# Token sums of squares added on VectorE, and another order around the layer norm, in a two-block model kernel

## The reference

```python
def rms_norm(x, gain):                      # also _rmsnorm
    return x * rsqrt(mean(x * x, -1) + 1e-6) * gain

# first block: 16 meta tokens are put ahead of the 512, so L = 528
hn = rms_norm(h, attn_norm)
h = h + fox_mixer(hn)                       # attention, 16 heads of 64, gated; ends with o @ w_out
h = h + (silu(n @ W_gate) * (n @ W_up)) @ ffn_w_out     # n = rms_norm(h, ffn_norm), hidden 2816
x = rms_norm(h, final_norm)[:, 16:]

# second block: c gives six vectors sh1, sc1, g1, sh2, sc2, g2 through w_ada
n1 = _rmsnorm(x, norm1_g) * (1 + sc1) + sh1
glu_in, z, xbc, dt_raw, gate_in = split(n1 @ w_in)
u_a, u_b = split(glu_in); u = u_a * sigmoid(u_b)
u = silu(_layernorm(causal_depthwise_conv(u, 31 taps)))  # subtract the token's mean, scale by rsqrt(var + eps)
y_cv = u @ w_cv_out
xbc = silu(causal_depthwise_conv(xbc, 4 taps))           # 2048 columns xs, 512 B, 512 C
y = ssd(xs, softplus(dt_raw + dt_bias), -exp(a_log), B, C) + d_skip * xs   # 32 heads, 4 groups, chunks of 64
y = _rmsnorm(y * silu(z), per group of 512)
g_cv, g_ssm = split(sigmoid(gate_in))
x = x + g1 * ((g_cv * y_cv + g_ssm * (y @ w_ssm_out)) @ w_mix_out)
n2 = _rmsnorm(x, norm2_g) * (1 + sc2) + sh2
x = x + g2 * moe(n2)                        # 64 experts of hidden 512 in 8 groups, top 2
return _rmsnorm(x, final_g)
```

## Time and profile before

| | before |
|---|---|
| time, median of 3 runs | 2719.16 us (2712.14 to 2720.99) |
| time of the profiled execution | 2708.46 us |
| its span | 2706.6 us |
| mean granted TensorE clock | 0.939 of full speed |
| busy: PE / DVE / ACT / POOL | 89% / 31% / 28% / 28% |
| chain that ended last, by engine | PE 56%, DMA 27%, DVE 10%, ACT 4%, issue 1% |
| its largest lines | DMA arena<-in_w 21%, L734 11%, L736 11%, L735 11%, L1240 7%, L2102 4%, L789 3% |
| DMA, mean over the span | 221 GB/s |
| DMA in slices 26 to 39 of 40 | 422 to 426 GB/s |

### The profile page before, as it was taken

The page is one execution under the profiler, slowest core; times in us unless marked ns, Lnnn a source line. Parts: engine busy times, 40 slices in busy tenths (PEclk is TensorE's granted clock), DMA queues, the critical chain, the costliest instruction groups (busy, mean ns, idle before and its releaser), DMA issues.

```text
span 2706.6 us, 27116 instructions
## 1 busy us (share of the span) xinstructions
PE 2417.0 (89%) x11252; PEld 1513.6 (56%) x11252; DVE 828.7 (31%) x1354; ACT 753.4 (28%) x1201; POOL 767.2 (28%) x487
## 2 busy tenths in 40 slices
PE   8999789999999998689997998798888888888885
PEld 6677457778888786577776786332222222332221
DVE  1633551100003799316654422311111111111113
ACT  4433552322223333236655422200000000000001
POOL 3333443454543443143322461401001010011000
PEclk9999899999998999699998899899999999988997
DMA  4253212532323332132333325799999999999995
GB/s 166 100 185 126 76 36 94 173 122 78 125 70 101 94 94 86 44 124 95 109 125 129 150 96 225 267 423 426 426 426 426 426 426 426 424 424 424 425 422 215
DMA packets 165051, 597.33 MB, mean 221 GB/s; under 512 B 15875, under 2 KB 81411, under 8 KB 139328
## 3 DMA queue, kind: packets, MB, share of 16 engines
q1 hardware_dynamic: 148320, 562.23, 53.3%
q10 hardware_dynamic: 5936, 23.90, 2.3%
q0 software_dynamic: 10672, 9.46, 1.1%
HBM read 591.01 MB, written 28.96 MB: 229 GB/s over the span
## 4 chain that ended last, share of the span: by engine, by line
PE 56%; DMA 27%; DVE 10%; ACT 4%; issue 1%; POOL 0%; SPq 0%; ACTq 0%; DVEq 0%; POOLq 0%
DMA arena<-in_w 21%; PE ps L734 11%; PE ps L736 11%; PE ps L735 11%; PE ps L1240 7%; DVE ps L2102 4%; DMA ring<-in_w 3%; PE ps L789 3%; PE ps L1238 2%; PE ps L1259 2%; ACT arena L1342 1%; DMA ring<-in_w_ada 1%; PE ps L818 1%; PE ps L808 1%; PE ps L761 1%
## 5 line engine op out<-in xcount | busy, mean ns | idle before, releaser
L2497 POOL TENSOR_TENSOR ring_r<-ring,ring_r 128x1024 fp32r<-128x1024 f32 (+2 forms) x220 | 514.2, 2342 | 802.9 <-ACT ring_r L1331 802.8
L734 PE MATMUL ps<-r,ring_r 128*128 128x512 f32 (+1 forms) x1552 | 622.5, 401 | 9.7 <-ACT arena L1342 4.9
L735 PE MATMUL ps<-r,ring_r 128*128 128x512 f32 (+1 forms) x1552 | 610.8, 394 | 0.0
L736 PE MATMUL ps<-r,ring_r 128*128 128x512 f32 (+1 forms) x1552 | 610.6, 393 | 0.0
L1342 ACT ACTIVATE arena<-ps 128x512 f32<-128x512 f32 (+4 forms) x279 | 187.9, 693 | 1234.9 <-PE ps L1240 868.8
L1240 PE MATMUL ps<-arena 128*64 128x512 f32 x672 | 326.7, 644 | 79.5 <-DMA arena<-in_w 79.4
L734 PEld LDWEIGHTS ps<-r,ring_r 128*128 128x128 f32 (+1 forms) x1552 | 294.3, 190 | 81.5 <-issue 18.7
L1238 PE MATMUL ps<-arena 128*64 128x512 f32 x672 | 332.9, 644 | 0.0
L735 PEld LDWEIGHTS ps<-r,ring_r 128*128 128x128 f32 (+1 forms) x1552 | 294.2, 190 | 65.2 <-issue 3.7
L736 PEld LDWEIGHTS ps<-r,ring_r 128*128 128x128 f32 (+1 forms) x1552 | 293.5, 189 | 64.6
L1331 ACT ACTIVATE ring_r<-ring 128x1024 fp32r<-128x1024 f32 (+2 forms) x220 | 222.8, 1014 | 332.4 <-PE ps L736 231.0
(11 more groups left out here) (329 smaller groups left out, 2370.9 us busy)
## 6 DMA issues: line engine op xcount, KB each, us to landing
arena<-in_w SPq DMA_DIRECT2D x105, 2048.0 KB, 35.9
ring<-in_w SPq DMA_DIRECT2D x87, 2048.0 KB, 37.1
ring<-in_w_ada SPq DMA_DIRECT2D x12, 2048.0 KB, 12.8
ring<-in_ffn_w_in SPq DMA_DIRECT2D x22, 1024.0 KB, 7.7
ring<-in_w_in SPq DMA_DIRECT2D x40, 512.0 KB, 5.8
ring<-in_fox_w_in SPq DMA_DIRECT2D x8, 2048.0 KB, 8.2
ring<-in_w_in SPq DMA_DIRECT2D x8, 2048.0 KB, 9.6
ring<-in_ffn_w_out SPq DMA_DIRECT2D x4, 2048.0 KB, 7.9
```

Source lines behind the costliest of these rows:

```text
L734: e.matmul(out, wh[:, k, :], X.hi[:, k0 + k, :], start=first and k == 0, stop=False)
L735: e.matmul(out, wh[:, k, :], X.lo[:, k0 + k, :], start=False, stop=False)
L736: m = e.matmul(out, wl[:, k, :], X.hi[:, k0 + k, :], start=False, stop=last and k == nk - 1)
L2497: e.tensor_tensor(GL[t], grans[t][1], GH[t].bitcast(F32), ALU.subtract).then_inc(sem["gr_lo"], 1)
```

## The change

- **Squares added up by VectorE.** For all of these norms VectorE adds the rows of squares elementwise (`add_squares`, L1853) into one row, `ACC[0]` (which is `RST`), except the last. TensorE then does one `sums_by_token`: for each 128 tokens the accumulated row and the last row of squares against ones, 8 matmuls instead of 32 (24 instead of 64 for "fin" with accumulators `RST` and `CBM`). The sums no longer stand between the tiles of op, of the feed-forward block's output and of n2. Row k's squares wait for the add of row k - 2.
- **ada(8)** stands after op5 instead of after op7.
- **The output weights of the feed-forward block** come in four loads of 256 columns for each half instead of two of 512 columns split by rows, and the tiles follow: both parts (k 0 to 7, 8 on) of a tile behind each other instead of four tiles' first parts and then their second parts.
- **The start.** SyncE issues the first half (256 columns) of the first weight load before the input rows have landed, the second half after both.
- **Around the layer norm.** The last step's 4-tap convolution (xbc 6 and 7) runs ahead of the last 31 taps. All six gate tiles eg0 to eg5 stand on TensorE ahead of conv_sum 6 and 7; behind these xbc 8 and 9 ahead of the sums of "ln", xbc 10 around the spread, xbc 11 after it, then the transposes sb and the pair co0 and co1. The mean is evicted to a buffer of its own (`MEAN`, in CBM). The scans of dt stand behind the adds.

The diff, cut to its core ("..." marks what is left out; the other norms' calls change like those shown):

```diff
--- before.py
+++ after.py
@@ bank_table: the banks from the taps on (the other stages alike) @@
     t("eg", 0, skip=held)
+    t("eg", 1, skip=held)
     t("acc", skip=held)
-    t("eg", 1, skip=held)
+    for nt in range(2, NG):
+        t("eg", nt, skip=held)
+    t("xbc", 8)
+    t("xbc", 9)
+    t("ln")
+    t("xbc", 10, skip={ps("ln").bank})
+    t("lnb")
...
@@ weight_table @@
-        for c in range(2):
-            block(a["ffn_w_out"], 512 * c, r0=128 * k0)
-            block(a["ffn_w_out"], 512 * c, r0=128 * (k0 + 8), nk=n - 8)
+        for c in range(4):
+            ap = load((0, (n, 256), wrows(a["ffn_w_out"], 128 * k0, n, 256 * c, 256)))[:, :n * 256].rearrange("p (k n) -> p k n", k=n)
+            for j in range(2):
+                for k in (slice(0, 8), slice(8, n)):
+                    grans.append((len(loads) - 1, ap[:, k, 128 * j:128 * j + 128]))
...
     tiles(*[8224 + 128 * i for i in range(4, NG)])
+    block(a["w_in"], 4096)
     for c in range(2):
         block(a["w_cv_out"], 512 * c)
...
@@ build_program @@
+        ACC = [RST, CBM[:, 0:512]]
+        MEAN = CBM[:, :]
...
+        def square_of(name, k, i=0):
+            return ACC[i] if k == 0 else TMP[i if name == "fin" else k % 2]
...
@@ pe @@
-            def sum_row(name, j, nk, off=0):
...
-                for tt in range(4):
-                    rows = TMP[j % 2][:, off + 128 * tt:off + 128 * tt + 128]
...
+            def sums_by_token(name, off=0):
+                rows0, adds0, nk = sums[name]
+                many = n_sums.get(name, 1)
+                u = ps(*name) if type(name) is tuple else ps(name)
+                w.wait_ge(sem["sq"], rows0 + many * nk)
+                w.wait_ge(sem["sq_used"], adds0 + many * (nk - 2))
+                w.wait_ge(u.free, u.n)
+                both = [[square_of(name, k, i) for k in (0, nk - 1)] for i in range(many)]
+                for tt in range(4):
+                    at = slice(off + 128 * tt, off + 128 * tt + 128)
+                    for x in both[0]:
+                        m = e.matmul(u.ap[:, tt:tt + 1], x[:, at], ones[:, 0:1], start=x is both[0][0], stop=x is both[0][1])
+                    if many == 2:
...
             for nt in range(8):
                 whole("op", nt, X=XO)
-                if nt % 4 == 3:
-                    ada(7 + nt // 4)
-                if nt >= 2:
-                    sum_row("fn", nt - 2, 8)
-            sum_row("fn", 6, 8)
-            sum_row("fn", 7, 8)
+                if nt in (3, 5):
+                    ada(7 + nt // 5)
+            sums_by_token("fn")
...
-                for c in range(2):
-                    for r in (0, 8):
-                        for j in range(4):
-                            u = ps("fo", half, 4 * c + j)
+                for c in range(4):
+                    for j in range(2):
+                        u = ps("fo", half, 2 * c + j)
+                        for r in (0, 8):
                             tile(u.ap, XH[half], u, k0=r, first=r == 0, last=r == 8)
...
             whole("eg", 0, X=X1)
+            whole("eg", 1, X=X1)
             conv_sum(4)
             conv_sum(5)
...
-            whole("eg", 1, X=X1)
+            for nt in range(2, NG):
+                whole("eg", nt, X=X1)
+            conv_sum(6)
+            conv_sum(7)
+            whole("xbc", 8, X=X1)
+            whole("xbc", 9, X=X1)
+            sums_by_token("ln")
+            whole("xbc", 10, X=X1, between={2: lambda: spread("ln", "lnb")})
+            whole("xbc", 11, X=X1)
             u = ps("sb")
...
-            whole("eg", 2, X=X1)
+            pair([ps("co", 0), ps("co", 1)], XC)
             ub, u = ps("sb"), ps("sc")
...
-            conv_sum(6)
-            conv_sum(7)
-            whole("eg", 3, X=X1)
-            sum_rows("ln", 8)
-            fill(2, "lnb")
-            spread("ln", "lnb")
-            whole("eg", 4, X=X1)
-            whole("eg", 5, X=X1)
-            pair([ps("co", 0), ps("co", 1)], XC)
             for nt in range(2, 8):
                 whole("co", nt, X=XC)
...
-            for j in range(4):
-                whole("xbc", 8 + j, X=X1)
             for g in range(4):
...
@@ act @@
-            def square_row(name, k, src, n, gain=1.0):
-                rows0, sums0 = sums[name]
-                if k >= 2:
-                    w.wait_ge(sem["sq_used"], sums0 + k - 1)
-                e.activation(TMP[k % 2][:, :n], src, ACT.Square, scale=gain).then_inc(sem["sq"], 1)
+            def square_row(name, k, src, n, i=0, gain=1.0):
+                rows0, adds0, nk = sums[name]
+                if name == "fin":
+                    if k >= 2:
+                        w.wait_ge(sem["sq_used"], adds0 + 2 * (k - 2) + i + 1)
+                elif k >= 3:
+                    w.wait_ge(sem["sq_used"], adds0 + k - 2)
+                e.activation(square_of(name, k, i)[:, :n], src, ACT.Square, scale=gain).then_inc(sem["sq"], 1)
...
+            for nt in range(NG):
+                early_gate(nt)
+            evict(MEAN, ps("red"), ACT.Copy, scale=1.0 / D)
...
@@ dve @@
+            def add_squares(name, k, n=T, i=0):
+                rows0, adds0, nk = sums[name]
+                many = n_sums.get(name, 1)
+                w.wait_ge(sem["sq"], rows0 + many * k + i + 1)
+                if k >= 2:
+                    w.wait_ge(sem["sq_used"], adds0 + many * (k - 2) + i + 1)
+                acc = ACC[i][:, :n]
+                e.tensor_tensor(acc, acc, square_of(name, k, i)[:, :n], ALU.add).then_inc(sem["sq_used"], 1)
...
+                if q == 3:
+                    short_conv(2 * q, [Cf[:, nt - 4, :] for nt in pair], accs)
+                    w.wait_ge(sem["xbc"], 8)
                 for i in range(31):
...
-            for c in range(4):
-                sl = slice(c * 128, (c + 1) * 128)
-                e.tensor_tensor_scan(DT[:, 2, sl], C("ones", 0, 32), DT[:, 1, sl], 0.0, ALU.mult, ALU.add).then_inc(sem["acs"], 1)
             u = ps("red")
...
             for k in range(8):
-                e.tensor_tensor(cv[:, k, :], cv[:, k, :], RST[:, :T], ALU.subtract).then_inc(sem["cvc"], 1)
...
+                e.tensor_tensor(cv[:, k, :], cv[:, k, :], MEAN, ALU.subtract).then_inc(sem["cvc"], 1)
+                if k >= 2:
+                    add_squares("ln", k - 1)
...
@@ sp @@
-            for i in range(3):
-                w.wait_ge(sem[f"in{i}"], 16)
...
+            (dst, src), = loads[0].parts
+            e.dma_start(dst[:, :, 0:256], src[:, :, 0:256]).then_inc(loads[0].slot, 16)
+            for i in range(3):
+                w.wait_ge(sem[f"in{i}"], 16)
+            w.wait_ge(loads[0].slot, 16)
+            e.dma_start(dst[:, :, 256:512], src[:, :, 256:512]).then_inc(loads[0].slot, 16)
```

More of the change, by code:

```diff
@@ L134, in state_tiles @@
 def state_tiles():
-    out = [("xbc", 8 + j) for j in range(4)]
+    out = []
     for g in range(4):
@@ L215, in bank_table @@
             t("fo", half, nt)
-            if half == 1 and nt == 4:
-                t("fin")
+    t("fin")
     t("finb")
@@ L454, in granule_uses @@
             whole("hu", nt)
-        for c in range(2):
-            for _ in range(4):
-                partly()
-            for j in range(4):
-                whole("fo", half, 4 * c + j)
+        for nt in range(8):
+            partly()
+            whole("fo", half, nt)
     for q in range(4):
@@ L466, in granule_uses @@
         whole("eg", nt)
+    for nt in range(8, 12):
+        whole("xbc", nt)
     for nt in range(8):
@@ L724, in granule, with tile @@
                 return t, GH[t], GL[t]
-            def tile(out, X, use, k0=0, first=True, last=True):
+            def tile(out, X, use, k0=0, first=True, last=True, between={}):
                 t, wh, wl = granule()
```

208 lines of the change are left out of this document (103 added, 105 removed).

## The result

The changed kernel takes 2672.08 us (median of four runs, 2671.10 to 2675.39), the kernel before beside it 2715.65 (2709.91 to 2720.99): a ratio of 0.9841, interval 0.9821 to 0.9860, some 43 us less. (Less than 2%, but clear of the noise.) The forecast was 2672.0. That the two agree to a tenth is chance: the profiled executions, from the first of which the sum was read, took 2708.46 and 2671.73, so they are 36.7 apart where the sum said 47.0, and the kernel before varies by itself (2705 to 2725 in all runs beside the experiments, with medians of 2711 to 2719). What follows goes by the traces.

What follows compares the result with a forecast made beforehand. A chain of waits bounds the kernel: TensorE's products, VectorE's taps, then expert loads. Terms 4.2 + 1.2 + 0 + 38.7 + 0 + 2.9 = 47.0 us off the median give 2672, range 2652 to 2695.

Steps and rivals of the forecast that it cites:

- What a saved us is worth: Stages ahead of the expert loop: what they save moves the whole loop, one for one; a 38.84 us stall stands there.
- Start: First norm, "x": root at about 18.5 instead of 22.67, inputs delayed by 2.5; gain 4.2 us (2 to 7).
- Output projection: Norm "fn": 4.1 us of squares out, new wait of 3 to 4.5 for ada(8)'s load; +1.2 (-1.5 to +2.5).
- fin: End of the feed-forward block: 8.5 us of rows out, longer tail at the lower clock; taken as 0, between -0.4 and +4.9.
- Layer norm: Convolution to state space stage: mean 13.9 us earlier, sums 1.8 us, pair co0, co1 34.0 earlier at 1126.0.
- xbc 11 to 1125.4: After the layer norm's sums: TensorE runs xbc 10 to 1120, xbc 11 to 1125.4, then the pair at 1126.0.
- Behind co7: Third z tile 38.8 us after co7 instead of 43.9, 5.1 saved; with the pair's part, gain 38.7 us (33 to 42).
- no needed cover: Rival denied: without the xbc tiles behind co7 TensorE idles and its clock halves; gain 20 us, 2699, chance 0.03.
- gn: Groups of the state space stage: fewer passes, but an add in the chain; 0 us (-3 to +4).
- n2: The norm "n2": 4.1 us of squares out, tail 1.2 longer for the last add; +2.9 us (0 to 4).
- The point figure: Whole kernel: 2672 us, the summed gain of 47.0 taken from the median of the runs shown.
- The case named the likeliest: Whole kernel: the forecast itself, gains of 33 to 56 us, chance 0.60.

Runs made afterwards that it cites:

- sp_late: Changed kernel with the first half of the first weight load issued behind the inputs' landing again, as before the change: 2670.42 us.
- fin_fill: Changed kernel with twelve filler matmuls where TensorE idles ahead of the token sums of "fin": 2671.69 us.
- pool3: Changed kernel with GpSimd splitting three granules (xbc 11, co0, co1) ahead of its low parts of the layer norm's rows instead of behind: 2660.57 us.
- xbc11_late: pool3 with xbc 11 moved from between the spread and the pair co0, co1 to behind co7: 2654.88 us.
- after_again: The changed kernel itself, run and profiled once more on the same chip as the variants: 2672.10 us (2667.61 to 2679.13).
- ada_first: Changed kernel with ada(8) left behind op5 but its load ahead of the first piece of the feed-forward weights in SyncE's list: 2662.93 us.
- start_root: xbc11_ada with the first weight load behind the inputs and ScalarE's granule copies behind the root: 2654.66 us.
- xbc11_ada: xbc11_late with ada(8) behind op7 again: 2647.55 us, ratio 0.9747 to the kernel before the change.
- ada_back: Changed kernel with ada(8) behind op7 again on TensorE, ScalarE and VectorE (the output projection's repair): 2665.39 us.

## Why the prediction was right, and where it was not

- **What a saved us is worth:** right; 37.0 us at the loop's first matmul, 36.7 at the end. But the 38.84 us of the earlier trace rows were misread as a stall. They are one load's time in the chain; TensorE's own waits from 1760 us on are at most 3.9 us each, before and after.
- **Start:** +4.2 said, root 22.67 to 18.61, of which 3.0 reach the first product tile. The delay of the inputs was said as 2.5. The slowest input took 9.9 to 10.3 us in three profiles with the early load and 8.2, 8.3 and 9.2 in those without it, so it is 0.7 to 2.1. sp_late shows that it costs nothing, since the granule copies behind it would wait as long.
- **Output projection:** the step failed. Said +1.2, measured -6.8, and the repair takes 11.2 out of the stretch. The wait was seen and nearly sized (5.41 for 3 to 4.5). Missing was the clock behind it. To the end of the sums it took 46.4 us where 37.8 were said: the load 20.4 for 19.4, ada(8) 6.1 for 3.8, the two tiles 14.1 for 10.9, the tail 5.8 for 3.7 (its sums 3.54 us, at 0.50 again). Some 7 us of that are the lower clock, which was priced for "fin" and left out here.
- **"fin":** 0 said, +2.8 measured; the idle (5.94 for 6.1) and the sums (10.4) came as forecast, the removed rows gave 2 us more. The reason given, the idle ahead, explains only some 2 us of it: fin_fill took the idle away and the clock fell all the same, as it had in the kernel before.
- **Layer norm:** mean evicted at 1096.03, for 1099.3 less the 2.4 gained ahead; adds 0.69; sums 1.84 for 1.8. Up to xbc 10 each step holds. Then "xbc 11 to 1125.4" failed: the sum set two of GpSimd's splits between the adds, and never looked where they stand in GpSimd's own order. They stand behind its low parts, which cost 11.36 us and a slow tile and put the pair at 1135.49 where 1126.0 - 2.4 was said. pool3 has them where the sum had them: pair at 1125.14, and VectorE's held instructions cost TensorE 3.3 us, within the up to 4.4 that the sum had for two splits.
- **Behind co7:** the z tile follows 38.8 us after co7's end (1179.94 to 1218.70): as said. That the xbc tiles were no needed cover was right, and xbc11_late shows that one of them is free there.
- **"gn", "n2":** +1.0 and +3.8 for 0 and +2.9.
- **The point figure** was right by luck. The sum, 47.0, is 10 too many by the two profiles, and 3 too many for the medians, 43.6 here and 44.4 beside after_again. It was taken from 2719.16, the median of the three runs then known, 3.5 above the 2715.65 with the fourth, and 10.7 above the profiled execution that its terms were read from. The case named the likeliest held, in the lower half of its 33 to 56.
- **Against the Trainium skill:** the rule of its page "SBUF — State Buffer" ("Who interferes with whom"), that VectorE and GpSimd lock each other out of a shared port, agrees with the durations in both directions here, 2.88 for 0.69 and 6.21 for 2.40, but the changed kernel itself escaped it where the sum feared it. The rule of its page "TensorE: Matmul & The Clock Gate" ("What's actually happening"), that an idle engine falls back to half its clock, doesn't cover what fin_fill and the kernel before show: 1.00 to 0.50 within sums that run without a gap.

## What to carry to other kernels

When work is put into another place of one engine's order, follow its helpers to every engine that prepares it: here ScalarE's copies had been moved along and GpSimd's splits had not, and a count of three granules in that engine's code was worth 11 us. When a matmul is moved ahead, its load must come ahead too, and so must what the engines behind it wait for: ada_first moved only the load. A wait can cost the lower clock behind it as well. Read a variant by milestones in the trace, and have a second profile of the same kernel: in ada_first and start_root the time moved by more than the edited stretch did, once because the edit reached further than meant, once where the edit touches nothing.

## What the runs showed of the hardware that was not expected

A GpSimd split of 2.40 us took 6.21 while VectorE ran subtractions and adds out of SBUF without a gap (the same in all five profiles with pool3's edit, 6.20 to 6.22), and the scans behind them took 3.46 for 1.35: either engine can be held by the other.

TensorE's granted clock fell from 1.00 to 0.50 (2.4 to 1.2 GHz) within matmuls of one or two columns that ran without a gap: in the kernel before it was busy for 2.00 of 2.00 us in each window of the fall.

The same wait can cost the clock or not. Ahead of ada(9) TensorE waited 3.39 us (the changed kernel) and 3.13 (xbc11_ada), and ada(9) ran at full speed, 1.92 us; with 3.15 (ada_back) it took 3.64.
